# Thirty row sums moved out of the even block, and the norm's sums as wide products

## The reference, cut to what matters

```
m = silu(c) @ w_mod[l] + b_mod[l]          # 6 * 1024 numbers for each of layers l = 0, 1
hl = rmsnorm(xl, norm1_g) * (1 + scale) + shift          # shift and scale are parts of m
xc = rmsnorm(ctx, norm1_g) * (1 + cscale) + cshift       # the context, modulated from silu(c_ctx)
_, ctx_state = rglru(xc @ w_in[:, 512:1024], h0 = 0)     # even layer: only the final state is kept
proj = hl @ w_in                                         # gate, LRU input, three Hyena inputs
y_a = gelu(gate) * rglru(proj[:, 512:1024], ctx_state)
z = v; for o in 0, 1: z = gates[o] * fftconv(z, filter[o])
```

## Time and profile before

| | us |
|---|---|
| median of 3 runs (2921.5 to 2925.46) | 2923.77 |
| the profiled execution, whole | 2930.76 |
| its span, first to last instruction | 2929.0 |
| TensorE busy in it | 2467.4 (84%) |
| VectorE busy in it | 1283.7 (44%) |
| even block | 1217.65 to 1409.3 |
| filters' stage up to its first tap product | 1409.36 to 1438.91 |
| RWKV scan | 353.2 to about 602 |

### The profile page before, as it was taken

The page is one execution under the profiler, slowest core; times in us unless marked ns, Lnnn a source line. Parts: engine busy times, 40 slices in busy tenths (PEclk is TensorE's granted clock), DMA queues, the critical chain, the costliest instruction groups (busy, mean ns, idle before and its releaser), DMA issues. The chain is left out here.

```text
span 2929.0 us, 42537 instructions
## 1 busy us (share of the span) xinstructions
PE 2467.4 (84%) x18510; PEld 1528.2 (52%) x18510; DVE 1283.7 (44%) x2087; ACT 591.5 (20%) x858; POOL 243.2 (8%) x159
## 2 busy tenths in 40 slices
PE   4996499978999999788774978998987787889897
PEld 3785299956545545566332743343435574434343
DVE  4876755544323323388677441112126743112212
ACT  3332401023111111253410220010013242100001
POOL 2000000012000000220124110000001111000000
PEclk7997599988999999898777989999998888999999
DMA  4581011132999999437110359999972145999996
GB/s 156 165 281 48 22 47 33 33 147 94 417 418 418 416 407 417 180 128 231 59 43 0 146 231 426 427 428 428 427 298 74 42 179 235 427 427 428 428 427 268
DMA packets 121146, 725.33 MB, mean 248 GB/s; under 512 B 11942, under 2 KB 65446, under 8 KB 83943
## 3 DMA queue, kind: packets, MB, share of 16 engines
q1 hardware_dynamic: 92776, 695.27, 58.7%
q10 hardware_dynamic: 28224, 27.92, 2.9%
HBM read 721.06 MB, written 2.10 MB: 247 GB/s over the span
## 5 line engine op out<-in xcount | busy, mean ns | idle before, releaser
L2018 PE MATMUL ps<-s_ring,s_c_XG 128*64 128x512 f32 x2048 | 468.7, 614 | 85.7 <-DMA s_ring<-in_exp_w 62.6
L2018 PEld LDWEIGHTS ps<-s_ring,s_c_XG 128*64 128x64 f32 x2048 | 162.8, 141 | 385.6 <-issue 384.6
L2130 DVE TENSOR_TENSOR s_c_hid<-ps,s_c_sil 128x512 f32<-128x512 f32 x32 | 34.4, 1074 | 514.7 <-PE ps L2018 514.7
L356 PE MATMUL ps<-s_h_part,s_w_hi 128*128 128x512 f32 x624 | 197.6, 399 | 46.9 <-PEq L459 41.9
L2059 PE MATMUL ps<-s_ring,s_c_hidT 128*64 128x512 f32 x1024 | 223.6, 594 | 0.0
L2018 PE MATMUL ps<-s_ring,s_m_XG 128*64 128x512 f32 x1024 | 222.8, 593 | 0.0
L356 PEld LDWEIGHTS ps<-s_h_part,s_w_hi 128*128 128x128 f32 x624 | 119.6, 193 | 76.8 <-issue 47.7
L2018 PEld LDWEIGHTS ps<-s_ring,s_m_XG 128*64 128x64 f32 x1024 | 72.8, 137 | 142.7 <-issue 141.6
L2059 PEld LDWEIGHTS ps<-s_ring,s_c_hidT 128*64 128x64 f32 x1024 | 72.2, 137 | 137.5 <-issue 136.5
L356 PE MATMUL ps<-s_src_part,s_w_hi_at 128*128 128x512 f32 x384 | 126.1, 411 | 0.8 <-DVE s_src_part L1568 0.8
L356 PE MATMUL ps<-s_h_part,s_w_lo 128*128 128x512 f32 x312 | 123.6, 396 | 0.0
(11 more groups left out here) (621 smaller groups left out, 4301.8 us busy)
## 6 DMA issues: line engine op xcount, KB each, us to landing
s_ring<-in_exp_w SPq DMA_DIRECT2D x192, 2048.0 KB, 17.3
s_ring<-in_moe_w_gate SPq DMA_DIRECT2D x32, 2048.0 KB, 12.4
s_ring<-in_moe_w_up SPq DMA_DIRECT2D x32, 2048.0 KB, 15.3
s_ring<-in_moe_w_down SPq DMA_DIRECT2D x32, 2048.0 KB, 12.5
s_mod_w<-in_vectors SPq DMA_DIRECT2D x70, 512.0 KB, 4.5
s_mod_w_at<-in_vectors SPq DMA_DIRECT2D x42, 512.0 KB, 4.6
s_w_raw<-in_w_in ACTq DMA_DIRECT2D x11, 1024.0 KB, 7.5
s_w_raw_at<-in_w_in ACTq DMA_DIRECT2D x8, 1024.0 KB, 6.1
```

What stands on the lines that cost most here:

```text
L356: last = nc.tensor.matmul(bank, w[a][:, i % 2, k, c0:c0 + P], x[b][:, k, at], start=start, stop=stop)
L2018: last = nc.tensor.matmul(ps[x * SLOTS:(x + 1) * SLOTS, bank + fh, :], XG[:, k, c0:c0 + SLOTS], w[x][:, at:at + 512], start=(k == 0), stop ...
L2130: nc.vector.tensor_tensor(hid_out[:, fh * per:(fh + 1) * per, :], ps[:, UP + fh, :].rearrange("s (p j) -> s p j", j=nj), sil[:, fh * 512:( ...
```

## The change

Layer 1's 42 row sums are split: 21 (chunks 6 to 26) go into the RWKV scan, 12 (27 to 38) stay in the even block, 9 (39 to 47) go into the filters' stage. The scan's sums now have three buffers and two silu rows (`c` and `c_ctx`) at fixed addresses, in free memory. `beside` says after which job they run: one after RB and BT as before, two after the last Z of a step, one after the first U of the second direction. In the filters' stage six run between the two `hidden` calls and three after the second; `th` lies over their buffers, so ScalarE's first tanh waits for all nine; the loads of the first three stand in SP's queue ahead of the tables, the others behind them.

In the even block's start the eight squares are summed by eight products with two columns as the stationary side and 512 moving ones, into two partitions; ScalarE copies them out, and four small products turn them back. GpSimd loses the low part of unit 0 to VectorE; its memset and the low part of unit 1 now come after the context's low parts; ScalarE's high part of unit 1 comes before its copy.

```diff
-MOD_EARLY = 6
+MOD_EARLY, MOD_SCAN, MOD_EVEN = 6, 27, 39
...
+            def beside(job):
+                name, j, d, l = job
+                if name in ("RB", "BT"):
+                    return 1
+                if name == "Z" and d == 1 and l == TOP and j + 1 < N_STEP:
+                    return 2
+                return int(name == "U" and d == 1 and l == 1 and j > 0)
...
-                            if name in ("RB", "BT"):
-                                u = 2 * j + (name == "BT")
-                                later.vector(dve, u, u + 1)
+                            n_side = beside(job)
+                            if n_side:
+                                u = sided
+                                sided += n_side
+                                later.vector(dve, u, u + n_side)
...
-                        for k in range(4):
-                            sums_of(k)
+                        for k in range(KD):
+                            pe.wait_ge(squared.sem, k + 1)
+                            last = nc.tensor.matmul(ps[0:2, self.SUMS, :], pair[:, k, :], square[:, k, :], start=(k == 0), stop=(k == KD - 1))
+                        last.then_inc(summed.sem, 1)
                         pe.wait_ge(ctx_diag.sem, 1)
...
-                        for k in range(4, KD):
-                            last = sums_of(k)
+                        pe.wait_ge(sums_here.sem, 1)
+                        for t in range(KT):
+                            last = nc.tensor.matmul(ps[:, self.SPREAD_X, 2 * t:2 * t + 2], two[0:2, t * P:(t + 1) * P], ident[0:2, 0:2], start=True, stop=True)
                         last.then_inc(summed.sem, 1)
...
+                        W.split_hi(act, 1)
+                        act.wait_ge(summed.sem, 1)
+                        nc.scalar.activation(two[:], ps[0:2, self.SUMS, :], ACT.Copy).then_inc(sums_here.sem, 1)
                         for k in range(KD):
                             act.wait_ge(ctx_h.sem, k + 1)
...
                         V.tensor_tensor(diag_c[:], bcast(ident, N_CT), rstd_c[:].unsqueeze(2).to_broadcast([P, N_CT, P]), ALU.mult).then_inc(ctx_diag.sem, 1)
-                        for k in range(6, KD):
-                            square_of(k)
+                        W.split_lo_unit(dve, 0)
...
                         M.all_done(dve)
-                        finish_modulation(1)
...
-                        nc.gpsimd.memset(pad[:], 0.0).then_inc(*pool_out.up())
-                        W.split_lo(pool, 0, 1)
                         for k in range(KD):
                             pool.wait_ge(ctx_hi.sem, k + 1)
                             nc.gpsimd.tensor_tensor(hc_parts[1][:, k, :], hc[:, k % HC, :], hc_parts[0][:, k, :].bitcast(F32), ALU.subtract).then_inc(ctx_lo.sem, 1)
+                        nc.gpsimd.memset(pad[:], 0.0).then_inc(*pool_out.up())
                         W.split_lo(pool, 1, 2)
...
+            M = Modulation(None, "2", [(1, m, 0) for m in range(MOD_EVEN, MOD_COLS)], at=(at["th"], (at["th"] + 4 * MOD_BUFS * D,)))
...
+                    M.load(sp, 0, MOD_BUFS)
                     for dst, src in ((w3[:], A["filt_w3_2"]), (win[:], A["hy_window"].rearrange("(t p) c -> p t c", p=P)),
                                     (spec[:], A["hy_spectrum"].rearrange("(t p) f -> p t f", p=P))):
                         sp.dma_start(dst, src).then_inc(*tables_in.up(16))
+                    M.load(sp, MOD_BUFS)
...
+                    M.silu_of_c(act)
                     for j in range(n_j):
                         gate(0, j, r, "lru_br_2")
...
+                    act.wait_ge(M.step.sem, len(M.jobs))
                     for j in range(n_j):
                         nc.scalar.activation(th[:, j, :], r[:, j, :], ACT.Tanh, scale=rate[:, 1, j:j + 1]).then_inc(*act_out.up())
...
                     hidden(0, "filt_b1_2")
+                    M.vector(dve, 0, 6)
                     dve.wait_ge(f_sin.sem, 1)
                     hidden(1, "filt_b2_2")
+                    M.vector(dve, 6, len(M.jobs))
                     dve.wait_ge(f_sin.sem, 2)
                     V.memset(hid[H:H + 1, :], 1.0).then_inc(f_hid.sem, 1)
+                    M.all_done(dve)
+                    finish_modulation(1)
                     for t in range(KT):
                         window(0, t)
```

More of the change, by code:

```diff
@@ L375, in __init__, with load @@
                 self.silu = signal(f"mod{tag}_silu")
[L377 to L380, removed]
+            def load(self, sp, first=0, end=None):
+                for j in range(self.n_c if first == 0 else 0):
+                    at = vec_at["c_2_row"] + (self.c_first + j) * D
+                    sp.dma_start(self.c[j][:], A["vectors"][:, at:at + D]).then_inc(self.c_here.sem, 16)
+                for u in range(first, len(self.jobs) if end is None else end):
+                    l, m, _ = self.jobs[u]
                     if u >= self.bufs:
@@ L386, in silu_of_c @@
             def silu_of_c(self, act):
-                act.wait_ge(self.c_here.sem, 16)
-                nc.scalar.activation(self.c[:], self.c[:], ACT.Silu).then_inc(self.silu.sem, 1)
+                act.wait_ge(self.c_here.sem, 16 * self.n_c)
+                for j in range(self.n_c):
+                    nc.scalar.activation(self.c[j][:], self.c[j][:], ACT.Silu).then_inc(self.silu.sem, 1)
             def vector(self, dve, first, end):
@@ L394, in vector @@
                     if u == 0:
[L395 removed]
+                        dve.wait_ge(self.silu.sem, self.n_c)
                     dve.wait_ge(self.here[u % self.bufs].sem, 16 * (u // self.bufs + 1))
@@ L905, in rwkv_scan @@
                 pe_did, dve_did, act_did, pool_did = (signal("rw_" + n) for n in ("pe", "dve", "act", "pool"))
-                later = Modulation(st, "_ctx", side, 2)
+                later = Modulation(st, "_ctx", side, at=(SCAN_AT["mod_w"], SCAN_AT["mod_silu"]))
                 with nc.Block() as block:
@@ L2343, in run @@
                 total_c, ms_c, root_c, rstd_c = (few.take("ctx_" + n, [P, N_CT]) for n in ("total", "ms", "root", "rstd"))
-                zero = few.take("even_zero", [1, 2 * KT])
+                two = place("even_two", at["two"], [2, T])
                 e = few.take("rate_e", [P, n_j])
@@ L2388, in _ @@
                     def _(pe):
[L2389 to L2393, removed]
                         def product(i):
@@ L2510, in _ @@
                     def _(dve):
-                        V.memset(zero[:], 0.0)
                         V.memset(pair[:, :, 0:1], 1.0)
@@ L2523, in _ @@
                         V.tensor_scalar(ms_c[:], total_c[:], 1.0 / D, RMS_EPS, ALU.mult, ALU.add).then_inc(ctx_ms.sem, 1)
-                        for k in range(4, 6):
+                        for k in range(4, KD):
                             square_of(k)
@@ L3204, in build @@
                 xa = sbuf(lru, "xa", [P, CT, T])
-                N.run(cat[:, 0:CT, :], xa, hy, gates, rate, state, [(1, m, 0) for m in range(MOD_EARLY, MOD_COLS)])
+                N.run(cat[:, 0:CT, :], xa, hy, gates, rate, state, [(1, m, 0) for m in range(MOD_SCAN, MOD_EVEN)])
                 lru_and_filters(xa, gates, rate, state, cat[:, 0:CT, :], spec, Kc, Ks, EVEN_AT)
```

22 lines of the change are left out of this document (11 added, 11 removed).

## The result

The changed kernel takes 2903.25 us (median of five runs, 2899.38 to 2909.17), the kernel before 2925.09 beside it: a ratio of 0.9928 with a 95% interval of 0.9909 to 0.9948, 21.8 us less. The forecast was 24.0 less. The profiled execution took 2909.01, with a span of 2907.1 instead of 2929.0.

What follows compares the result with a forecast made beforehand. TensorE (84% busy) was taken to hold the even block only while it works, with pauses behind VectorE's row sums. 27.6 + 2.8 - 6.2 - 0.2 = 24.0 us saved gives 2899.8 us, range 2896 to 2903, with rivals 2891 to 2908.

Steps and rivals of the forecast that it cites:

- The even block from the gates on: Even block behind the gates: with 12 of 42 sums left, pauses, slow restarts and tail shrink, 27.6 us saved.
- the pause at the first LRU gate: Even block: TensorE's 7.55 us wait for ScalarE to take the first LRU gate out of PSUM; forecast to stay.
- The three pauses: Even block: TensorE's waits for the weights' low part on VectorE, behind row sums; forecast to go, 15.3 us.
- the slow restarts: Even block: TensorE's slow-clock tiles behind two of the long pauses; forecast to go, 3.0 + 1.8 = 4.8 us.
- the tail: Even block's end, last product to next stage: forecast to shrink from 10.51 to 3.0 us, saving 7.5 us.
- The block's start: Even block's start: wide norm sums raise the clock after about 5 us and the low chain ends earlier, 2.8 us saved.
- the clock stays low: Rival, even block's start: no clock rise under the wide sums, loses 1.3 us; 19.9 saved in all, 2903.9; chance 0.17.
- the even block keeps a pause: Rival, even block: another wait ends last where the low parts did, 20 saved instead of 27.6, 2907.4; chance 0.07.
- The filters' stage: Filters' stage: nine added sums, late rows and GpSimd's SBUF work delay the first tap product; costs 6.2 us.
- hidden after all: Rival, filters' stage: chunks early enough and GpSimd not in the way, so 30.2 us saved, 2893.6; chance 0.25.
- The scan: RWKV scan: 21 more sums fit VectorE's idle places while TensorE sets the pace; costs 0.2 us, bounds 0 and 1.
- the scan pays for its sums: Rival, scan: jobs behind new sums lie on TensorE's path, L1024 waits return; 7.2 us slower in all, 2931.0; chance 0.04.

Runs made afterwards that it cites:

- even_42: Changed kernel with all 30 moved sums back in the even block (42 there); even block 185.4 us, ratio 0.9987 to the kernel before.
- thin: Changed kernel with the norm sums as 32 narrow products, all ahead of the turning; even block 165.5 us, ratio 0.9974 to the kernel before.
- lo_pool: Changed kernel with unit 0's low part and the pad's memset on GpSimd ahead of the context's low parts; ratio 0.9947 to the kernel before.
- rows_first: Changed kernel with the filters' nine row loads ahead of the three tables in SyncE's queue; stage 32.9 us, ratio 0.9927 to the kernel before.
- scan_sums: Changed kernel with all sums, but the scan's 21 layer-one loads bring one partition of 128; scan 244.4 us, ratio 0.9906 to the kernel before.
- scan_none: Changed kernel without the scan's 21 layer-one sums and their loads; scan 245.0 us, ratio 0.9928 to the kernel before.
- scan_loads: Changed kernel with all scan loads, but its 21 layer-one sums over 8 of 1024 elements; scan 250.5 us, ratio 0.9934 to the kernel before.
- filt_to_even: Changed kernel with the filters' nine sums in the even block too (21 there); median 2897.33 us, ratio 0.9910 to the kernel before.
- first_16: Changed kernel with the filters' nine sums in the even block and ten scan sums in the first projection's stage; 2908.58 us, ratio 0.9936 to before.
- scan_quarters: Changed kernel with each scan row load as four 128 KB transfers, held apart from the fifth row on; scan 273.5 us, ratio 0.9986 to before.

## Why the prediction was nearly right

**The even block from the gates on: right in mechanism, 27.6 forecast, 25.8 measured** by even_42; in the changed kernel itself 28.3 us of the gain lie behind the pause at the first LRU gate. The three pauses, the slow restarts and the tail went, and the 8.9 us pause stayed, as the prediction had it. The tail is 3.1 us for 3.0.

**The block's start: 2.8 forecast, 2.8 in the changed kernel, 5.3 by even_42** (190.7 - 185.4). Counted from the first norm product, the low chain ended after 36.0 us before, 33.4 in the changed kernel and 31.8 in even_42, held by GpSimd's low part as forecast (one L2559 of 3.25 us); the pause at the first LRU gate ended after 70.4, 67.6 and 66.2 us. The 1.4 us that even_42 has over the changed kernel go with its clock, which rose 2.7 us after the first wide product, not 6.0; that is the luck of one execution. Another 1.1 us of even_42's gain lie behind the pause. The prediction's working has a slip of 0.3: 1241.7 + 0.3 + 9.6 is 1251.6, not 1251.9. The clock rose under the wide products after 6 us, as assumed (5). That they and not the new order give the start's gain is shown by thin (+5.9) and lo_pool (-0.6). thin is not the kernel before, which had half its sums behind the turning. The rivals "the clock stays low" and "the even block keeps a pause" are out.

**The filters' stage: 6.2 forecast, 6.1 measured, by partly other reasons.** Forecast was a second `hidden` 3.4 us late for its rows, slowed by GpSimd, and then sums of 2.1, 2.1 and 1.6 beside it. Measured were 7.5 us of waiting for the fourth row, a `hidden` that began 6.0 us late and was slowed, and sums of 1.21 that slowed GpSimd instead. Two errors cancelled, which was luck. The rows_first run shows that the rows' and the tables' loads compete: whichever stands behind is late. The rival "hidden after all" is out.

**The scan: the step that failed.** "TensorE sets its pace ... I take 0.2; the bounds are 0 and 1" asked only whether a sum fits into VectorE's idle places and whether its row is there in time. Both hold, and scan_sums shows the sums at nothing. But 21 loads cost: four profiles without them (before, scan_none, scan_sums, even_42) have scans of 244.4 to 250.0, mean 246.8; six with 21 whole loads as in the change (after, scan_loads, filt_to_even, thin, lo_pool, rows_first) 250.5 to 257.6, mean 255.7. That is 8.9 us. About half of it, 4.5 us, stands in the five steps at full clock (means 145.8 and 150.3 for the same ten profiles, 144.7 to 147.2 against 148.3 to 151.8), and there scan_loads and scan_sums show the loads as the cause. Of the rest 3.7 us stand in the first two steps and 0.7 in the last. In the first two the ranges overlap (66.5 to 69.5 and 65.2 to 74.3), and the clock is at its lower level for 14 to 31 us of them; whether the loads cost time there is not settled. The rival "the scan pays for its sums" had the place right and the cause and price wrong.

**The sum.** 25.8 + 5.3 - 6.1 - 8.9 = 16.1 us are traced to the change's steps, 21.8 were measured. The missing 5.7 us stand in stages whose code is the same: 4.1 up to the scan, 2.1 behind the taps. In all experiments but first_16 the scan starts at 343.9 to 349.1, in the one profile of before at 353.2. That execution was 5.7 us above the median of its kind, the profiled one of after 5.8 above its own, so the medians keep the gap. Whether the kernel before is always slow there is open; one profile of it can't tell. The scan's 9.4 in the profiled pair, for the 8.9 of the means, makes up the small rest. So the total was near in spite of a step that was wrong by 9 us, and that nearness is luck.

## What to carry to other kernels

A place that is idle on the engine is not free for that: the loads for its work run beside all else that the DMA queues bring, instructions included. In a stretch of thousands of small products on TensorE, count the loads that run beside it, and try them where TensorE runs long instructions: in the even block nine more sums with 4.7 MB of rows cost nothing. When an experiment holds a transfer back, check that what waits for it isn't late in its turn, as in scan_quarters. Before moving work out of a stage, find out how much of it the stage can keep: here 21 of 42 sums were free, and 27 cost 3.5 us.

## What the runs showed of the hardware

- The profile lists instruction packets in a DMA queue of their own. In the scan one came every 3.7 us where no row load was near; beside or just behind a row load (144 packets; if they are spread evenly over 16 engines, 9 of 159 ns each, an estimate of 1.4 us) it came at 4.4 us, and behind packets of 4.6 us or later TensorE stopped for 0.4 to 1.2 us. The Trainium skill (Runtime: NRT & Kernel Launch, Instruction fetch mechanics) says that instructions are refilled in blocks of 16 KiB while the current ones run, and that this is mostly hidden. The packets' size agrees; hidden throughout it is not here: 7 stops, 4.0 us, in 151.1.
- The Trainium skill (DMA: Bandwidth & Descriptors, Queues, rings and completion order) has each DMA engine take turns between its queues, a group of some descriptors at a time. A mean delay of 0.7 us beside loads of 1.4 would fit; no run here shows the turns themselves, and scan_quarters, whose stops have another cause, doesn't test them.
- With two-column stationary tiles and 512 moving columns running, the granted clock went from 0.50 to 1.00 in 2.6 to 6.0 us (twelve profiles); with 128 stationary and 2 moving columns it was still 0.50 after 13.7 us of unbroken work (one profile, thin).
- When an operation on VectorE and a two-input operation on GpSimd overlapped, the loser changed: VectorE took 1.63 us for 0.68 in the sine's argument and 2.19 for 1.22 in the sixth sum; beside the last three sums, at 1.21 each, one operation of GpSimd took 4.87 for 1.27.
